# Moving 72 modulation units out of the third layer's heads into two feed-forwards

## The reference, cut to what is computed

```python
mod_x = (silu(c) @ w_ada[i] + b_ada[i])       # 1024 -> 6 * 1024, also for c_ctx
sh1, sc1, ga1, sh2, sc2, ga2 = split(mod_x, 6)
x = x + ga1 * mixer(rms_norm(x, g1) * (1 + sc1) + sh1)
x = x + ga2 * ffn(rms_norm(x, g2) * (1 + sc2) + sh2)
```

## Time and profile before

| | |
|---|---|
| median of 3 runs | 2457.93 us (2453.07 to 2458.34) |
| the profiled execution's own time | 2458.92 us |
| span of the profile | 2457.1 us |
| TensorE busy | 2321.8 us, 94% |
| VectorE / ScalarE busy | 54% / 42% |
| mean granted TensorE clock | 0.974 of full speed |
| mean DMA busy share | 41% |

### The profile page before, as it was taken

The page is one execution under the profiler, slowest core; times in us unless marked ns, Lnnn a source line. Parts: engine busy times, 40 slices in busy tenths (PEclk is TensorE's granted clock), DMA queues, the critical chain, the costliest instruction groups (busy, mean ns, idle before and its releaser), DMA issues.

```text
span 2457.1 us, 35805 instructions
## 1 busy us (share of the span) xinstructions
PE 2321.8 (94%) x14174; PEld 1891.9 (77%) x14174; DVE 1331.9 (54%) x2270; ACT 1039.2 (42%) x1954; POOL 33.6 (1%) x40
## 2 busy tenths in 40 slices
PE   5999999999898999899999999999999899998999
PEld 3656688888757999767666787688888787798999
DVE  4544433333655555567776434534344678756665
ACT  3443422222544444454445523423323555655543
POOL 0300000000200000000000000000000000000000
PEclk8999999999999999899999999999999899999999
DMA  7564433333345665244554322333223221154554
GB/s 277 175 219 153 139 105 109 103 103 103 112 162 182 207 204 175 84 146 157 195 173 162 106 98 88 129 97 109 86 95 104 85 86 61 61 171 138 181 189 138
DMA packets 94885, 335.96 MB, mean 137 GB/s; under 512 B 10624, under 2 KB 12672, under 8 KB 94464
## 3 DMA queue, kind: packets, MB, share of 16 engines
q1 hardware_dynamic: 94720, 333.67, 40.2%
HBM read 332.58 MB, written 1.05 MB: 136 GB/s over the span
## 4 chain that ended last, share of the span: by engine, by line
PE 84%; DVE 6%; DMA 4%; ACT 4%; issue 3%; SPq 0%; ACTq 0%; DVEq 0%
PE out L1162 23%; PE out L1163 23%; PE out L1164 23%; DMA raw<-stream 4%; PE sc L1241 2%; PE pt L1251 1%; ACT w_hi L1306 1%; PE pv L1267 1%; PE aux L1187 1%; PE pt L1141 1%; PE out L1141 1%; DVE w_lo L1549 1%; PE aux L1172 1%; PE pv L1265 1%; PE sc L1141 1%
## 5 line engine op out<-in xcount | busy, mean ns | idle before, releaser
L1162 PE MATMUL out<-act_hi,w_lo 128*128 128x512 f32 (+1 forms) x2208 | 777.3, 352 | 29.2 <-DVE act_lo L1724 19.2
L1163 PE MATMUL out<-act_lo,w_hi 128*128 128x512 f32 (+1 forms) x2208 | 763.6, 346 | 0.0
L1164 PE MATMUL out<-act_hi,w_hi 128*128 128x512 f32 (+1 forms) x2208 | 763.0, 346 | 0.0
L1306 ACT CAST w_hi<-raw 128x1024 fp32r<-128x1024 f32 (+2 forms) x444 | 453.0, 1022 | 419.2 <-PE out L1164 411.2
L1549 DVE TENSOR_TENSOR w_lo<-raw,w_hi 128x1024 fp32r<-128x1024 f32 (+2 forms) x444 | 530.0, 1196 | 172.9 <-ACT w_hi L1306 172.4
L1162 PEld LDWEIGHTS out<-act_hi,w_lo 128*128 128x128 f32 x2208 | 423.9, 192 | 91.5 <-issue 31.0
L1164 PEld LDWEIGHTS out<-act_hi,w_hi 128*128 128x128 f32 x2208 | 423.3, 192 | 50.6
L1163 PEld LDWEIGHTS out<-act_lo,w_hi 128*128 128x128 f32 x2208 | 424.1, 192 | 47.8
L1162 PE MATMUL out<-mix_hi,w_lo 128*128 128x512 f32 (+1 forms) x1120 | 378.9, 338 | 4.3 <-issue 1.6
L1163 PE MATMUL out<-mix_lo,w_hi 128*128 128x512 f32 (+1 forms) x1120 | 377.3, 337 | 0.0
L1164 PE MATMUL out<-mix_hi,w_hi 128*128 128x512 f32 (+1 forms) x1120 | 377.2, 337 | 0.0
(11 more groups left out here) (205 smaller groups left out, 2015.3 us busy)
## 6 DMA issues: line engine op xcount, KB each, us to landing
raw<-stream SPq DMA_DIRECT2D x604, 512.0 KB, 3.6
raw<-stream SPq DMA_DIRECT2D x16, 384.0 KB, 3.2
raw<-stream SPq DMA_DIRECT2D x16, 256.0 KB, 2.6
x<-xin SPq DMA_DIRECT2D x1, 2048.0 KB, 11.7
consts<-const SPq DMA_DIRECT2D x1, 1344.0 KB, 10.2
x<-ctx SPq DMA_DIRECT2D x1, 1024.0 KB, 6.0
out<-x SPq DMA_DIRECT2D x8, 128.0 KB, 1.7
consts<-const SPq DMA_DIRECT2D x1, 320.0 KB, 11.2
```

Of the source, the lines that this page charges most:

```text
L1162: nc.tensor.matmul(ps, wl, xh, start=(k == 0), stop=False)
L1163: nc.tensor.matmul(ps, wh, xl, start=False, stop=False)
L1164: ins = nc.tensor.matmul(ps, wh, xh, start=False, stop=(k == s.nk - 1))
L1306: nc.scalar.copy(w_hi[:, number % HL, 0:n], raw[:, place[number] % RAW, 0:n]).then_inc(S["hi_ready"], 1)
```

## The change

Layer 2's own 32 units (its banks 1 and 2) go to layer 0's feed-forward, behind the 8 already there, in the score bank as those. Of layer 3's 48 units, 40 were in layer 2's heads and 8 in the gap of its second norm; now the first 8 are in that gap and 40 in layer 2's feed-forward, in `ptb[1]`. Layer 2's heads have none. T and the transposes of values in layer 2 alternate between both banks, as in layer 3. The number of units, blocks and loads is the same.

```diff
@@ plan
-            pt, free = take("pt", 2 if item.first or item.layer == 3 else 1, ev)
+            pt, free = take("pt", 2, ev)
...
-        s.pt, s.pt_free = take("pt", 1 if made.layer == 2 else 2, s.ev)
+        s.pt, s.pt_free = take("pt", 2, s.ev)
...
-    def ffn(layer, n, fill, next_n):
+    def ffn(layer, n, fill, next_n, psum="sc"):
...
-        spread(todo[3:], [lambda a=a: ada(*a) for a in fill])
+        spread(todo[3:], [lambda a=a: ada(*a, psum=psum) for a in fill])
...
-    ffn(0, NT, ada_list(1, [1])[8:], NT)
+    ffn(0, NT, ada_list(1, [1])[8:] + ada_list(2, [1, 2]), NT)
     layer_first(1, ada_list(1, [2]), 2, ada_list(2, [0])[:8])
     ffn(1, NX, ada_list(2, [0])[8:], NT)
-    layer_second(2, ada_list(2, [1, 2]) + ada_list(3)[:40], gap=ada_list(3)[40:])
-    ffn(2, NT, [], NT)
+    layer_second(2, gap=ada_list(3)[:8])
+    ffn(2, NT, ada_list(3)[8:], NT, psum="pt")
```

## The result

The changed kernel takes 2496.39 us (median of 4 runs, 2495.66 to 2496.93) against 2455.5 (4 runs, 2448.03 to 2458.34); the medians are 40.9 us apart. The two profiled executions lie 36.7 us apart in their own times (2495.66 and 2458.92) and in their spans (2493.8 and 2457.1). The profile of before is one of the kernel's longer executions: the part before anything changed, up to the first row-sum matmul (L1172) behind layer 0's attention, took 252.8 us in it and 246.9 in the changed kernel's. So the 5.9 us are scatter of the start, and the stages have to be compared one by one.

The account below looks back on a forecast made before the run. TensorE, at work for 94% of the span, was taken to bound the kernel, without holes in the feed-forwards. 2458.92 + 51.9 (feed-forwards and norm) - 16.5 (heads) = 2494.3 us, range 2472 to 2503, chance 0.80.

Parts of the forecast that it names:

- What bounds the kernel: TensorE is never free in both feed-forwards; at the ends of heads 2 to 6 a VectorE and ScalarE chain sets the pace.
- A unit's price in a feed-forward, 0.75: Each unit between feed-forward blocks costs 0.75 us: +24.0 in layer 0, +29.3 in layer 2.
- The norm behind layer 2's feed-forward, -1.4: The last unit, behind the last block, keeps TensorE at work before the norm: -1.4 us, bounds 0 and -1.4.
- Banks and ring at nothing: In layer 2's feed-forward, five more finished banks and 72 loads cost nothing; uncovered banks 13 us, load waits up to 0.75 each.
- The second bank at nothing: Alternating T and value transposes between two banks in layer 2 gains 0, as no T waits for ScalarE's copy.
- What the heads give back, 16.5 in all: Layer 2's heads shorten by 16.5 us: 23.7 coming back, less 7.2 for the clock.
- the 13 to 24 that I gave as the sign of being right: Layer 2's heads would be shorter by 13 to 24 us if the forecast held.
- new waiting for 29.3 forecast: In layer 2's heads, 29.3 us of the removable 53.0 would not come back, mostly as TensorE waiting for the chain.
- The clock, -7.2: In layer 2's heads, clock falls take back 1.1 x 5, and 1.7 at head 1: 7.2 us, bounds 0 and 10.2.
- a fall at each of five ends: The clock falls at the ends of heads 2 to 6, costing 1.1 us each after VectorE's chain hides some of 1.7.
- What is left of the heads: Before the clock's part, layer 2's heads give back 53.0 - 29.3 = 23.7 us.
- The sum: Whole kernel: 2458.92 of the profiled run + 51.9 for feed-forwards and norm - 16.5 for heads = 2494.3 us.

Follow-up runs that it names:

- c3: c2 plus six groups of four matmuls, without load or reader, at the end of each of heads 2 to 6: 2492.5 us, 1.0162 of the kernel before.
- c2: The changed kernel with the second bank taken away from layer 2 again, units staying in the feed-forwards: 2495.99 us, 1.0178 of the kernel before.
- e1: c3 plus four more fills in the second group of heads 0, 1 and 2: 2489.03 us, 1.0142 of the kernel before.
- e3: Kernel before with nine units per head, placed 0, 2, 1, 0, 1, 1, 2, 2, and feed-forward units of layers 0 and 1 in pairs: 2447.69 us, ratio 0.9978.
- c1: The changed kernel as it is, run again beside the kernel before: 2496.77 us against 2452.29, ratio 1.018.
- c4: The changed kernel with the feed-forwards' units in pairs, half as many places: 2478.91 us, 1.0105 of the kernel before.

## Why the prediction was right, point by point

- **What bounds the kernel.** Right. TensorE is full in both feed-forwards before and after, and at the ends of heads it isn't the engine that sets the pace (c3: 15.7 us of work put in, 5.3 us less).
- **A unit's price in a feed-forward, 0.75.** Right: the same 1.66 us in the timeline, and 24.5 and 29.9 us between the same matmuls of the blocks where 24.0 and 29.3 were forecast, 0.77 each; 0.79 by leaving out.
- **The norm behind layer 2's feed-forward, -1.4.** Wrong: from the first row-sum matmul to the first block it is 7.84 us after 8.09. The last unit does stand in front of it, and TensorE's wait for the sum is 1.88 us instead of 2.43, but the clock in the norm was 0.54 after 0.52. So a unit in that place is not what gives the norm behind layer 0's feed-forward its clock of 0.74; what does stays open.
- **Banks and ring at nothing.** Right. No unit between blocks waited for DMA, at a share of 0.43 and 144 and 146 GB/s, less than the 165 that I estimated.
- **The second bank at nothing.** Right (c2).
- **What the heads give back, 16.5 in all.** Too much: 11.1 us between the nine marks (312.2 to 301.1), also below the 13 to 24 that I gave as the sign of being right. With the rest of layer 2 up to its second norm it is 12.4. The chain of VectorE and ScalarE behind it was read rightly: 8.84 us, and 24.4 us of new waiting for 29.3 forecast (a slow S, 2.08 us for 1.13, takes some of it up).
- **The clock, -7.2.** The term that was too small, by 2.1: c3 and e1 give 9.3. These are 2.4 in head 0, 0.2 in each of heads 1 and 2, and 0.3, 2.4, 1.4 and 2.4 at the next ends, and somewhat more where the fills weren't hidden whole. The forecast of a fall at each of five ends was right for four. A fall there costs up to 2.4 us where I took 1.1, and the dearest that I hadn't priced is in head 0.
- **What is left of the heads.** 11.1 and 9.3 are 20.4, for 23.7 forecast before the clock's part. A small part of these 3.3 is that I priced all units at 0.54, where a pair costs 0.98 (two of c3's fills, 1254.98 to 1255.96 in its timeline). At the ends of heads 2 to 6 that error is in what leaves and in the new waiting alike and falls out of the difference; it counts for the six pairs of heads 0 and 1, 0.1 each, 0.6 together. The other 2.7 stay open, and heads of three kernels with the same number of units differ by more than that (132.8 to 137.4 us for the first three).
- **The sum.** 35.4 forecast; 36.7 between the profiles, 44 by the ratio. That the first two lie so near is luck: the heads gave back 5.4 less than forecast, the feed-forwards cost 2.7 more and the norm 1.2 more, and a start that was 5.9 us slow in the execution I summed from, with 2 us in other stretches, covered all but 1.3 of that. Against the timed runs of before, the change costs 44 us, and of these the forecast has four fifths. Summing from one execution carries that execution's scatter, and 1.0 above the median of three runs did not show it: 23 runs beside e1 to e3 had a median of 2452.6, 6.3 below it.
- **The rules of the Trainium skill.** That a loop which leaves TensorE idle between bursts is throttled again each time (TensorE: Matmul & The Clock Gate, HAM oscillation) agrees with four ends of heads in five, and not with the fifth, which stayed at 1.00. That rotating groups through PSUM banks overlaps evacuation (Perfetto Trace Analysis, Matmuls) changed nothing here, since no transposition waited for a bank (c2 and c1, 0.0002 apart).

## What to carry to other kernels

Small independent work belongs where the big engine waits for a chain of others, not where there is the most of the big engine's own work. In a full stretch it is paid for whole, with a surcharge for the change from one kind of matmul to another, and in the place that it has left, the waits that it hid come into the open. Before such a move, walk the chain of the other engines at the old place from its start to its end and compare it with the engine's own work there without the filler: here 9.0 us against 4.5 gave the direction and most of the size. Where small work must stand in a full stretch, put it in pairs (groups of three and more weren't tried). And before a sum is drawn up from one profiled execution, compare its stages with those of a second one: here a single stage was 5.9 us off.

## What the runs showed of the hardware that was not expected

- Work without purpose made the kernel faster: 30 groups of four small matmuls, 15.7 us busy, shortened the heads by 5.3 us, as the granted clock stayed at its upper level (1.00, 2.4 GHz) behind three ends of heads where it had fallen to 1.2 GHz for part of the time (0.66 over ten us).
- Four matmuls of 2 stationary columns between blocks cost 0.75 us, the next four 0.44. The block's second matmul behind them comes 0.34 us after its first, where 0.23 is the rule, whether there are four or eight.
- What a fall of the clock costs depends on the place and the length: 2.4 us in head 0 (0.57 against 0.86 over twelve us), 0.2 in each of heads 1 and 2, nothing at the end of head 2 (0.83 against 1.00 over ten), 1.6 at the end of head 6. It isn't always small in head 1 either: in c4, where ten us there are at 0.66, head 1's span is 46.7 us, against 45.1 in c3 with eight us at 0.79.
